# A seven-product feed-forward network in fp32 halves: other places for copies, weight sums and low halves, a fourth bank for the down product

## The reference, cut to what matters

```python
def mix_and_mlp(x, attn_o, conv_o, w_out, g_mix_post, g_mlp_pre, w_up, w_down, g_mlp_post):
    m = jnp.einsum('bte,ed->btd', jnp.concatenate([attn_o, conv_o], axis=-1), w_out)
    x = x + rmsnorm(m, g_mix_post)
    h = rmsnorm(x, g_mlp_pre)
    f = jnp.einsum('btf,fd->btd', jnp.square(jax.nn.relu(jnp.einsum('btd,df->btf', h, w_up))), w_down)
    return x + rmsnorm(f, g_mlp_post)
```

## Time and profile before

| what | us |
|---|---|
| three timed runs | 1787.22, 1791.11 (median), 1799.20 |
| the profiled execution | 1783.06 |
| its span, first to last instruction | 1781.3 |
| stage that the change touches | from 876.84 to the end |

### The profile page before, as it was taken

One profiled execution on the slowest core, in us unless ns is written; L12 is line 12 of the kernel. 1 busy time (PEld: TensorE's weight loads), 2 busy tenths in 40 slices (PEclk: granted clock), 3 DMA queues, 4 the chain that ended last, 5 costly groups with the idle time before them and its releaser, 6 DMA issues.

```text
span 1781.3 us, 24842 instructions
## 1 busy us (share of the span) xinstructions
PE 1525.5 (86%) x8928; PEld 1220.2 (69%) x8928; DVE 941.7 (53%) x1524; ACT 740.1 (42%) x1312; POOL 721.4 (41%) x658
## 2 busy tenths in 40 slices
PE   4798889989699998779858888888778899988997
PEld 2356436644588775458657777777767899888997
DVE  1226637778875442452655544554666544445445
ACT  3214628886157654643433333333324332233331
POOL 2232000123962211043545555645546455455452
PEclk8999989999899989979979999999989999999999
DMA  6011030513052004332132222222323321221213
GB/s 206 6 43 49 12 116 6 115 24 49 1 172 74 1 1 150 124 141 95 67 99 82 65 89 94 70 83 82 95 71 107 107 83 59 94 91 62 82 55 123
DMA packets 112248, 140.17 MB, mean 79 GB/s; under 512 B 15622, under 2 KB 97622, under 8 KB 109860
## 3 DMA queue, kind: packets, MB, share of 16 engines
q1 hardware_dynamic: 107532, 113.98, 21.0%
q0 software_dynamic: 4640, 25.18, 3.9%
HBM read 123.56 MB, written 15.90 MB: 78 GB/s over the span
## 4 chain that ended last, share of the span: by engine, by line
PE 23%; issue 13%; DVE 9%; POOL 9%; ACT 2%; DMA 1%; POOLq 0%; ACTq 0%; DVEq 0%; SPq 0%
PE ps L2407 8%; PE ps L2409 7%; PE ps L2408 7%; POOL dwlo L2134 3%; POOL uwA L2129 3%; POOL ring L2129 2%; DVE hlo L2685 1%; DVE moT L2672 1%; DVE moT L2678 1%; DVE moT L2591 1%; DVE xraw L2608 1%; ACT moT L2327 1%; DVE uraw L2597 1%; DVE xb L2601 1%; POOL uw L2129 0%
## 5 line engine op out<-in xcount | busy, mean ns | idle before, releaser
L2407 PE MATMUL ps<-hhi,dwhi 128*128 128x288 f32 (+3 forms) x736 | 247.3, 336 | 67.4 <-DVE hlo L2685 28.0
L2409 PE MATMUL ps<-hhi,dwlo 128*128 128x288 f32 (+3 forms) x736 | 243.0, 330 | 0.0
L2408 PE MATMUL ps<-hlo,dwhi 128*128 128x288 f32 (+3 forms) x736 | 243.0, 330 | 0.0
L2129 POOL TENSOR_TENSOR uwA<-uraw,uwA 128x512 fp32r<-128x512 f32 x96 | 133.0, 1399 | 253.5 <-ACT uwA L2228 253.5
L2134 POOL TENSOR_TENSOR dwlo<-draw,dwhi 128x1024 fp32r<-128x1024 f32 x62 | 151.3, 2450 | 128.2 <-ACT dwhi L2239 128.2
L2407 PEld LDWEIGHTS ps<-hhi,dwhi 128*128 128x128 f32 x736 | 139.1, 189 | 88.9 <-DVE moT L2760 23.7
L2760 DVE TENSOR_TENSOR moT<-ps,moT 128x288 f32<-128x288 f32 (+3 forms) x168 | 87.5, 533 | 202.3 <-PE ps L2409 202.3
L2407 PE MATMUL ps<-xb,uwA 128*128 128x256 f32 (+1 forms) x512 | 150.4, 294 | 27.8 <-ACT moT L2327 25.6
L2408 PE MATMUL ps<-xb,uwA 128*128 128x256 f32 (+1 forms) x512 | 149.3, 292 | 0.0
L2409 PE MATMUL ps<-xb,uwA 128*128 128x256 f32 (+1 forms) x512 | 148.7, 290 | 0.0
L2409 PEld LDWEIGHTS ps<-hhi,dwlo 128*128 128x128 f32 x736 | 139.1, 189 | 10.6
(11 more groups left out here) (328 smaller groups left out, 3737.9 us busy)
## 6 DMA issues: line engine op xcount, KB each, us to landing
uraw<-in_w_up SPq DMA_DIRECT2D x32, 1024.0 KB, 5.3
draw<-in_w_down SPq DMA_DIRECT2D x64, 512.0 KB, 3.4
x<-in_x SPq DMA_DIRECT2D x16, 512.0 KB, 3.6
w<-in_w_rows SPq DMA_DIRECT2D x2, 2048.0 KB, 10.5
w<-in_w_u SPq DMA_DIRECT2D x2, 2048.0 KB, 10.9
wo_raw<-in_w_out SPq DMA_DIRECT2D x8, 512.0 KB, 6.3
rows_d<-x SPq DMA_DIRECT2D x8, 512.0 KB, 2.6
up<-by_channel SPq DMA_DIRECT2D x32, 86.0 KB, 4.0
```

The costliest lines, as they stand in the source:

```text
L2129: nc.gpsimd.tensor_tensor(uw_of(i, 1), w_source(i), uw_of(i, 0), ALU.subtract).then_inc(s_wlo, 1)
L2407: nc.tensor.matmul(o, wh, xh, start=first, stop=False, skip_group_check=True)
L2408: nc.tensor.matmul(o, wh, xl, start=False, stop=False, skip_group_check=True)
L2409: return nc.tensor.matmul(o, wl, xh, start=False, stop=last, skip_group_check=True)
```

## The change

It edits the order and the waits of `phase_out_mlp`, and nothing in the count of matmuls:

- ScalarE does `take` of products 0 and 3 to 5 earlier against the casts of weights; `down_high` of d = 1 moves behind the copy of product 4 of unit 1, d = 2 behind four casts of the next group instead of two.
- `sums` of unit 1 begin ahead of the first `sum_hidden` on VectorE (three of the four), those of the next group's unit 0 ahead of the whole chunk loop, not behind its first chunk.
- `sum_hidden` step 2 reads bank 0 itself rather than the copy and runs ahead of `squared`; so product 0 of the next unit waits for that step.
- `down_low` of d = 2 and 3 moves from GpSimd to VectorE, behind chunks that `LOW_AFTER` names.
- The down product has four banks (4, 5, 1, 2), three in the last group. Its first three chunks do f = 0, 1 first, then f = 2, 3.
- The first group's unit 1 gets a raw buffer of its own, `uraw1`, loaded while the stage ahead ends. Final rows and transposes of `start` and `back` stand at other products; the rows 0 to 3 have four output buffers `y4`; `x_t1`, `x_high` and `x_low` of `turn` stand later.

```diff
-    DBANK = [4, 5, 1]
+    DBANK = {False: [4, 5, 1, 2], True: [4, 5, 1]}
+    EARLY = 3
+    LOW_AFTER = [{1: 2, 3: 3}, {3: 2, 7: 3}, {0: 2, 1: 3}]
...
+    def raw_of(p, g, j):
+
+        return uraw1 if p == 0 and j == 1 and isinstance(g, int) and g == 0 else uraw
...
+                if i == RT - 2:
+                    sp.wait_ge(s_wf, CC)
+                    load_up(0, 1, uraw1)
...
-            def down_low(p, g, d, last):
-                late = p == 1 and last
+                    nc.gpsimd.tensor_tensor(uw_of(i, 1), w_source(raw_of(p, g, j), i), uw_of(i, 0), ALU.subtract).then_inc(s_wlo, 1)
+
+            def down_low(p, g, d):
                 pool.wait_ge(s_dhi, grp(p, g, 4) + d + 1)
-                nc.gpsimd.tensor_tensor(dw_of(1, d, late), draw[d % 2][:], dw_of(0, d, late),
+                nc.gpsimd.tensor_tensor(dw_of(1, d, False), draw[d][:], dw_of(0, d, False),
...
-                more = not (p == 1 and last)
-                nxt = after(p, g, last)
-                if more:
+
+                if not (p == 1 and last):
+                    nxt = after(p, g, last)
                     up_low(*nxt, 0, (0, 1))
-                down_low(p, g, 2, last)
-                if more:
-                    up_low(*nxt, 0, (2, 3, 4))
-                down_low(p, g, 3, last)
-                if more:
-                    up_low(*nxt, 0, (5, 6))
+                    if back:
+                        store_final(1)
+                        inverse_rms(3, 2, s_q, s_r)
+                    up_low(*nxt, 0, (2, 3, 4, 5, 6))
...
-                up_high(p, g, 1, (0, 1, 2))
+                up_high(p, g, 1, (0, 1))
+                if back:
+                    square(0)
                 take(p, g, 0, 3, start)
-                up_high(p, g, 1, (3,))
                 if start:
                     first(RT - 1)
-                if back:
-                    square(0)
+                up_high(p, g, 1, (2, 3))
                 take(p, g, 0, 4, start)
                 up_high(p, g, 1, (4,))
                 take(p, g, 0, 5, start)
-                if back:
-                    square(1)
                 up_high(p, g, 1, (5,))
                 hid_high(p, g, 0, 0)
                 up_high(p, g, 1, (6,))
+
+                take(p, g, 1, 0, False)
+                if back:
+                    square(1)
                 hid_high(p, g, 0, 1)
-
-                take(p, g, 1, 0, False)
                 down_high(p, g, 0, last)
                 if turn:
                     x_high(1, 0)
-                down_high(p, g, 1, last)
-                if start:
-                    second(RT - 1)
+                take(p, g, 1, 3, False)
                 if back:
                     square(2)
-                take(p, g, 1, 3, False)
+                if start:
+                    second_square(RT - 1)
                 take(p, g, 1, 4, False)
+                down_high(p, g, 1, last)
+                take(p, g, 1, 5, False)
+                if start:
+                    second_scale(RT - 1)
+                hid_high(p, g, 1, 0)
+                hid_high(p, g, 1, 1)
+                if back:
+                    square(3)
+
+                more, nxt = not (p == 1 and last), after(p, g, last)
+                if more:
+                    up_high(*nxt, 0, (0, 1, 2, 3))
                 if turn:
                     x_high(1, 1)
-                take(p, g, 1, 5, False)
-                if back:
-                    square(3)
-                hid_high(p, g, 1, 0)
-                hid_high(p, g, 1, 1)
-
-                more, nxt = not (p == 1 and last), after(p, g, last)
-                if more:
-                    up_high(*nxt, 0, (0, 1))
-                if turn:
                     x_high(1, 2)
                 down_high(p, g, 2, last)
                 if more:
-                    up_high(*nxt, 0, (2, 3, 4))
+                    up_high(*nxt, 0, (4, 5, 6))
+                down_high(p, g, 3, last)
                 if turn:
-                    x_high(1, 3)
-                    x_high(1, 4)
-                down_high(p, g, 3, last)
-                if more:
-                    up_high(*nxt, 0, (5, 6))
-                if turn:
-                    x_high(1, 5)
-                    x_high(1, 6)
+                    for i in range(3, NP):
+                        x_high(1, i)
...
-                            pe.wait_ge(s_cp, N_CP + n4)
+                            pe.wait_ge(s_add, n4 - 1)
                     if i == 1 and not start:
                         pe.wait_ge(s_add, n4 - 3)
                         if j == 0:
-                            pe.wait_ge(s_ad, N_AD + down_base(p, g) - (1 if p == 1 and not first else 2))
+                            pe.wait_ge(s_ad, N_AD + down_base(p, g) - 1)
                     if i == 2:
                         if start:
                             pe.wait_ge(s_n, RT - 1)
                         else:
                             pe.wait_ge(s_add, n4 - 2)
+                            if j == 0:
+                                pe.wait_ge(s_ad, N_AD + down_base(p, g))
...
-                for q in range(3):
-                    part(q, range(FG - 1))
-                for q in range(3):
-                    part(q, range(FG - 1, FG))
-                for q in range(3, len(todo)):
+                for q in range(EARLY):
+                    part(q, range(2))
+                for q in range(EARLY):
+                    part(q, range(2, FG))
+                for q in range(EARLY, len(todo)):
...
+            def down_low(p, g, d, last):
+                late = p == 1 and last
+                dve.wait_ge(s_dhi, grp(p, g, 4) + d + 1)
+                nc.vector.tensor_tensor(dw_of(1, d, late), draw[d % 2][:], dw_of(0, d, late),
+                                        ALU.subtract).then_inc(s_dl2, 1)
...
-                    o, x, y = ct[:, 1, 1, 0:hw], s(2), s(0)
+                    o, x, y = ct[:, 1, 1, 0:hw], b(0), s(2)
...
+                if not start:
+                    sums(p, g, 1, range(3))
                 sum_hidden(p, g, 0, 0)
                 if start:
                     take_rows(RT - 3)
-                sums(p, g, 1)
+                    sums(p, g, 1, range(3))
+                sums(p, g, 1, (3,))
                 if start:
                     scale_mixed(RT - 1)
                 if back:
                     weigh_rows(0)
-                    finish_rows(0)
...
+                if not (p == 1 and last):
+                    sums(*after(p, g, last), 0, range(4))
...
-                    if q == 0 and not late:
-                        sums(*after(p, g, last), 0)
+                    if q in LOW_AFTER[p + late]:
+                        down_low(p, g, LOW_AFTER[p + late][q], last)
                     if turn:
-                        if q == 1:
+                        if q == 0:
+                            x_t1(1)
+                        if q == 2:
                             x_low(1, 1)
+                        if q == 3:
+                            x_low(1, 2)
+                        if q == 4:
+                            x_t3(1)
+                        if q == 5:
+                            x_t2(1)
+                            x_low(1, 3)
+                        if q == 6:
+                            x_t4(1)
+                            x_low(1, 4)
+                        if q == 7:
+                            x_low(1, 5)
+                            x_low(1, 6)
```

179 lines of the change are left out of this document (98 added, 81 removed).

## The result

| | us |
|---|---|
| changed kernel, four timed runs | 1728.51 median (1725.15 to 1730.15) |
| kernel before, four runs on the same chip | 1794.44 median (1787.22 to 1799.20) |
| ratio, 95% interval | 0.9634 (0.9593 to 0.9674): 3.7% faster |
| profiled execution of the changed kernel | 1729.3, span 1727.2 |

The forecast was 1731 with a range of 1695 to 1766.

What follows compares the result with a forecast made beforehand. TensorE sets the pace, the other engines matter where it waits. Gains of 27.3, 4.2, 12, 12.9 and 1.8 make 58 off the profiled 1783.1: 1725, plus 6 towards the median: 1731 us, range 1695 to 1766.

Steps and rivals of the forecast that it cites:

- Steady group of pass 0: Looped groups of pass 0: TensorE gaps fall from 8.6 us, gain 4.55 a group, six times 27.3.
- The port: VectorE operations with two SBUF inputs and GpSimd's exclude each other; `squared` of unit 1 takes 1.5 us or more.
- The rival without collisions: VectorE mostly gets the port first: pass 0 gains 6.4 us a group, 93 in all, 1697; chance 0.20.
- Start: Start group: product 5 can start about 891, not 900.31, product 6 waits for sums; gain 12 us.
- Turn and first group of pass 1: From the turn group's units through the next group's down product: gains 7 and 9.8, loss 3.9, together 12.9 us.
- chunk 0 behind sums and a final row: Down product of pass 1's first group: a TensorE wait of 3 us.
- chunk 8 behind `down_low`: Down product of pass 1's first group: a TensorE wait of 1.4 us.
- Pass 1: Looped groups of pass 1: gaps 4.8 against 5.5 us, gain 0.7 a group, six times 4.2.
- The wait of 1.8 at chunk 4: Down product of pass 1: chunk 4 wanted at 9.4 us after unit 1, chunk 0 added at 11.15.
- Lost in the seams: Start and turn give 9 us, not 25, chunk 4 waits 1.3 longer in 13 groups: 1764; chance 0.18.
- VectorE becomes the bound: VectorE's chain meets GpSimd more often, 6.5 us a group, 85 more: 1816, slower than before; chance 0.04.
- It does nothing for the pace: Gaps of copies go but come back whole at chunk 4: 1782, within 1%; chance 0.08.

Runs made afterwards that it cites:

- experiment 4: Changed kernel with GpSimd subtracting only 16 of 1024 columns of down weights d = 1 in groups 1 to 6 of each pass: 1707.39 us.
- Experiment 3: Changed kernel without the second raw buffer, the first group's unit 1 loading once GpSimd is through with unit 0: 1733.84 us, ratio 0.9669.
- Experiment 8: Changed kernel with four two-part first chunks, d = 2 cast earlier, sums behind `down_low(2)`, and final rows 2 and 3 at chunks 5 and 11: 1707.39 us.
- experiment 1: Kernel before with only the copies of product 3 and of unit 1's product 0 moved ahead of casts: 1788.88 us, ratio 0.9967.
- experiment 2: Changed kernel with the low down weights d = 2 and 3 back on GpSimd: 1750.47 us, ratio 0.9760.

## Why the prediction was right

**Steady group of pass 0: right, its parts nearly exact.** Forecast 46.4 from gaps of 0.15, 0.9 and 3.0. Measured 45.7 in the two groups at full clock, with 0, 0.78 and 2.74 (restarts of 0.16 included). The port was the step that this rested on: `squared` takes 1.85, and experiment 4 takes the port away and gets 0.68. The exclusion that the Trainium skill states (SBUF — State Buffer, "Who interferes with whom") is borne out here: `squared` ended 0.54 us behind the GpSimd operation that it met, nearly the whole 0.68 that it takes alone. The rival without collisions would have given 1697. The term that is missing is the clock: four groups took 47.4, which is 6.5 us in sum. So 26.2 stands for 27.3 by errors against each other: the groups at full clock came out 0.5 shorter than forecast (3.2 us for six), and the six before had taken 307.3 us, 2.1 more than six times the one that was read.

**Start: right, 14.6 for 12.** Product 6 was named as the one that waits, and it did, 5.92 us. The units got 16.0 us shorter, for 15.6 before the 3.5 that I took off, and the down product 1.4 longer, with a stretch at the lower clock in it. Experiment 3 corrects the reason: I gave the buffer `uraw1` for the whole gain at product 5, 9.3 us, and without it that product started 5.6 us later and the units were only 3 us longer.

**Turn and first group of pass 1: the sum right, one term wrong.** Chunk 4 of the turn waited 3.88 for 4.5, and the rest of the way to the next down product took 59.3 for 61. That down product was put at 32.6 and took 36.98. Two of its three terms came as forecast: `hlo` cost 1.99 for 2.5, and "chunk 0 behind sums and a final row" 2.93 for 3. The step that failed is the third, "chunk 8 behind `down_low`", 1.4: there was no wait at chunk 8, but one of 4.86 at chunk 11, behind final row 3, which is not in the sum at all, and a stretch at the lower clock with it. I had not laid out that row's load, which GpSimd issues behind the subtractions of seven up weights. Experiment 8 shows it.

**Pass 1: direction right, size half.** 0.65 and 2.2 were forecast at the two blocks, and 0.60 and 2.16 came. The wait of 1.8 at chunk 4 was too large. It was 1.27 in two of the six groups; in the other four the clock had fallen behind the 2.16, which made the chunks ahead longer by about as much, and there was no wait. All six took 52.3, for 53.0.

**The rivals.** "Lost in the seams" and "VectorE becomes the bound" did not come: VectorE is busy for 56% of the span, and where it is late it is one chain of seven operations, not its load. "It does nothing for the pace" is what experiment 1 measured for the copies alone, so its mechanism (gaps that come back at the next wait) was real; the other edits, `down_low` on VectorE above all (22 us in experiment 2), are what kept it from taking the whole change.

**What stays open.** Why the stage ahead of the changed one ran 8.5 us longer. Its stretch of 27.3 us at the lower clock is in the profile of the changed kernel and of the eleven experiments built on it, beginning at 650 to 655 us; the kernel before and experiment 1 have one of 3.4 us there. That looks as if it went with the change, but each of these two profiles is also of an unusually fast execution: 1783.06 us where the four timed beside the changed kernel took 1787 or more, and 1780.35, the fastest of experiment 1's ten. That one had a mean clock of 0.950, the nine others 0.941 to 0.944, and 24 us more at half the clock would be 0.007 less. So the long stretch may be usual without the change too. Only a profile of a usual execution of the kernel before would tell, and none is here. Also open is why the same gaps lower the clock in four groups of pass 0 and not in the other two; in experiment 3, with the same gaps, it was five.

## What to carry to other kernels

Lay out the chain that is late next, operation by operation with the time at which each engine comes free, before pricing a wait that goes: of the two copies' 3.6 us a group, 0.8 was left in pass 0 as long as the chain behind them was not moved too, and the clock took that. On an engine with a queue, put work that needs only a free slot ahead of work that needs another engine, and put nothing that waits for a load ahead of what empties a bank. And look at the granted clock of each repeated stretch, not only at its idle time: a gap of 2.7 us cost 1.6 more behind it in four groups of six.
